# A hybrid attention trunk on one core: two products over the compressed probabilities on GpSimd, the block choice and its mask's transposition in other steps

## The reference, cut to what matters

```python
# compressed keys (63 of them): softmax, kept for the choice of blocks too
p_cmp = masked_softmax(s_cmp, cmp_mask)
o_cmp = einsum('bsghc,bcgd->bsghd', p_cmp, vcmp)
# block choice: probabilities summed over the 4 heads of a group, gathered
# to 16 blocks of 64 keys; 8 blocks are chosen by top-k
imp = einsum('bsgc,cn->bsgn', p_cmp.sum(axis=3), overlap)
imp = where(valid, imp + FORCE_BONUS * forced, -1.0)
_, sel_idx = lax.top_k(imp, 8)
# o_sel: softmax over the chosen blocks; o_w: over a window of 512 keys
o = g[:, :, 0] * o_cmp + g[:, :, 1] * o_sel + g[:, :, 2] * o_w
```

## Time and profile before

| what | value |
|---|---|
| median of 3 runs | 3226.2 us (3223.99 to 3230.59) |
| the profiled execution: its own time | 3225.85 us |
| the profiled execution: span from first to last instruction | 3224.1 us |
| PE busy, share of the span | 97% |
| DVE busy | 61% |
| POOL busy | 52% |
| ACT busy | 34% |
| mean granted TensorE clock | 0.993 |

### The profile page before, as it was taken

The page is one execution under the profiler, slowest core; times in us unless marked ns, Lnnn a source line. Parts: engine busy times, 40 slices in busy tenths (PEclk is TensorE's granted clock), DMA queues, the critical chain, the costliest instruction groups (busy, mean ns, idle before and its releaser), DMA issues.

```text
span 3224.1 us, 40879 instructions
## 1 busy us (share of the span) xinstructions
PE 3125.8 (97%) x15015; PEld 2551.7 (79%) x15045; DVE 1979.9 (61%) x2633; ACT 1098.7 (34%) x1993; POOL 1675.7 (52%) x1781
## 2 busy tenths in 40 slices
PE   8999999998999999999999999989989999999998
PEld 6888887676788888888778888867668888888887
DVE  7882256887656666655578532578765655555555
ACT  2124314666312222222220342356651222222233
POOL 3457632233463556666745585222334566666665
PEclk7999999999999999999999999999999999999999
DMA  7444541001522222211234457200115221111112
GB/s 256 147 159 131 159 117 27 1 1 34 176 85 79 79 79 71 74 53 53 79 131 137 144 154 188 66 1 1 34 33 177 69 82 53 53 52 49 51 46 105
DMA packets 301358, 280.99 MB, mean 87 GB/s; under 512 B 11115, under 2 KB 275559, under 8 KB 300648
## 3 DMA queue, kind: packets, MB, share of 16 engines
q1 hardware_dynamic: 282002, 212.90, 22.6%
q10 hardware_dynamic: 19158, 65.47, 5.5%
HBM read 232.20 MB, written 38.80 MB: 84 GB/s over the span
## 4 chain that ended last, share of the span: by engine, by line
PE 88%; DVE 8%; ACT 2%; issue 2%; POOL 1%; ACTq 0%; DVEq 0%; POOLq 0%
PE lin L1451 47%; PE lin L1881 16%; PE lin L1598 8%; PE aux L1740 2%; DVE pTL L2643 2%; PE pv L1756 2%; PE lin L1716 1%; DVE negm L2619 1%; PE pv L1757 1%; PE lin L1787 1%; PE lin L1717 1%; PE pv L1556 1%; ACT pTH L2203 1%; PE lin L1682 1%; PE lin L1501 1%
## 5 line engine op out<-in xcount | busy, mean ns | idle before, releaser
L1291 POOL TENSOR_SCALAR unit<-wraw 128x512 fp32r<-128x512 f32 x340 | 286.9, 844 | 775.2 <-PE lin L1451 270.6
L1451 PE MATMUL lin<-hH,unit 128*128 128x512 f32 x1824 | 577.8, 392 | 0.1
L1451 PE MATMUL lin<-hL,unit 128*128 128x512 f32 x1824 | 573.5, 390 | 0.0
L1451 PE MATMUL lin<-hH,wlo 128*128 128x512 f32 x1824 | 572.9, 390 | 0.0
L1293 POOL TENSOR_TENSOR wlo<-wraw,unit 128x512 fp32r<-128x512 f32 x340 | 490.7, 1443 | 28.4
L1881 PE MATMUL lin<-fH,unit 128*128 128x512 f32 x1568 | 486.8, 390 | 5.3 <-DVE xT L2778 5.3
L2778 DVE SCALAR_TENSOR_TENSOR xT<-lin,adac,xT 128x512 f32<-128x512 f32 x448 | 328.7, 748 | 182.7 <-PE lin L1881 178.1
L1451 PEld LDWEIGHTS lin<-hH,wlo 128*128 128x128 f32 x1824 | 342.8, 188 | 72.3
L1451 PEld LDWEIGHTS lin<-hL,unit 128*128 128x128 f32 x1824 | 342.9, 188 | 71.8 <-issue 0.2
L1451 PEld LDWEIGHTS lin<-hH,unit 128*128 128x128 f32 x1824 | 339.5, 188 | 70.1 <-issue 1.9
L1881 PEld LDWEIGHTS lin<-fH,unit 128*128 128x128 f32 x1568 | 294.3, 188 | 68.2 <-POOL unit L1326 3.9
(11 more groups left out here) (353 smaller groups left out, 5715.1 us busy)
## 6 DMA issues: line engine op xcount, KB each, us to landing
wraw<-in_w_ff SPq DMA_DIRECT2D x136, 512.0 KB, 4.0
wraw<-in_w_ada SPq DMA_DIRECT2D x80, 512.0 KB, 3.9
wraw<-in_w_in SPq DMA_DIRECT2D x72, 512.0 KB, 4.9
mix_keep<-tmp ACTq DMA_DIRECT2D x32, 512.0 KB, 6.2
wraw<-in_w_o SPq DMA_DIRECT2D x24, 512.0 KB, 4.3
adar<-in_w_ada SPq DMA_DIRECT2D x16, 512.0 KB, 11.9
x_keep<-xT ACTq DMA_DIRECT2D x4, 2048.0 KB, 9.3
gate_keep<-ropes ACTq DMA_DIRECT2D x16, 512.0 KB, 3.6
```

The source lines that it names most:

```text
L1291: pool.tensor_scalar(high, raw, 1.0, 1.0, ALU.mult, ALU.mult).then_inc(w_hi, 1)
L1451: mm = pe.matmul(lin[c % 2][:, hf], w, m(k, hf), start=first, stop=last)
```

## The change

`cmp_probs` on DVE keeps only the sum, the reciprocal and the small gate product, and signals a new semaphore, for every tile but 7. POOL makes the one or two products over the probabilities in a new function, `compressed`, three steps after the c unit. The memset and the sum over the heads move to `cmp_sums`, which `select` calls. `select` itself moves from two steps after the c unit to five steps after it. The b group of tiles 6, 5 and 4 moves from one step before the end of the tile's first w set to three steps before; that of tile 7 stays. Two semaphores count over both layers where they counted for one.

```diff
-            steps[e - 1].append(dict(kind="b", qt=s["qt"]))
+            steps[e - (1 if s["qt"] == NT - 1 else 3)].append(dict(kind="b", qt=s["qt"]))
...
+                def compressed(qt):
+                    nth, n = NTH[qt], SEEN[qt]
+                    c3, r8 = cprob[:, :, 0:n], cst[:, 2, :].rearrange("p (h o) -> p h o", o=1).to_broadcast([P, NH, n])
+                    gate = gates[:, qt, 0:NH].rearrange("p (h o) -> p h o", o=1).to_broadcast([P, NH, n])
+                    pool.wait_ge(c_recip, (NT - 1) * layer + nth)
+                    pool.wait_ge(t_done, C_GROUP[qt + 1, NKV - 1]["no"] + 1)
+                    if qt >= CHOICE:
+                        pool_then(pool, pool.tensor_tensor(c3, c3, r8, ALU.mult))
+                    pool.tensor_tensor(cgated[:, :, 0:n], c3, gate if qt >= CHOICE else r8, ALU.mult).then_inc(c_gated, 1)
...
                     for u in range(len(STEPS)):
+                        if u >= 3 and u - 3 < len(UNITS) and UNITS[u - 3][0] == "c":
+                            compressed(UNITS[u - 3][1])
...
                 def cmp_probs(qt):
...
-                    gate = gates[:, qt, 0:NH]
-                    if qt < CHOICE:
-                        then(dve.tensor_tensor(r8, r8, gate, ALU.mult))
-                        gate = r8
-                    else:
-                        then(dve.tensor_tensor(c3, c3, bc(r8, n), ALU.mult))
                     if NTH[qt]:
-                        dve.wait_ge(t_done, C_GROUP[qt + 1, NKV - 1]["no"] + 1)
-                    dve.tensor_tensor(cgated[:, :, 0:n], c3, bc(gate, n), ALU.mult).then_inc(c_gated, 1)
-                    if qt < CHOICE:
+                        if qt < CHOICE:
+                            then(dve.tensor_tensor(r8, r8, gates[:, qt, 0:NH], ALU.mult))
+                        dve.sem_inc(c_recip, 1)
                         return
+                    then(dve.tensor_tensor(c3, c3, bc(r8, n), ALU.mult))
+                    dve.tensor_tensor(cgated[:, :, 0:n], c3, bc(gates[:, qt, 0:NH], n), ALU.mult).then_inc(c_gated, 1)
+
+                def cmp_sums(qt):
+                    n = SEEN[qt]
+                    dve.wait_ge(c_gated, NTH[qt] + 1)
                     then(dve.memset(psum4[:, :, :], 0.0))
                     p4 = cprob.rearrange("p (g i) c -> p g c i", g=NKV)[:, :, 0:n, :]
                     then(dve.tensor_reduce(psum4[:, :, 1:1 + n], p4, AX.X, ALU.add))
                 def select(qt):
+                    cmp_sums(qt)
...
-                    if 2 <= u < len(UNITS) + 2 and UNITS[u - 2][0] == "c" and UNITS[u - 2][1] >= CHOICE:
-                        select(UNITS[u - 2][1])
+                    if 5 <= u < len(UNITS) + 5 and UNITS[u - 5][0] == "c" and UNITS[u - 5][1] >= CHOICE:
+                        select(UNITS[u - 5][1])
```

More of the change, by code:

```diff
@@ L527, in trunk @@
         fin_low, o_hi, fin_lo = sem("fin_low"), sem("o_hi"), sem("fin_lo")
+        c_exp, c_recip = sem("c_exp"), sem("c_recip")
         sq_made, ss_added, ss_done = sem("sq_made"), sem("ss_added"), sem("ss_done")
@@ L1112, in layer_programs @@
             s_done, max_made, exp_made = (lsem(s) for s in ("s_done", "max_made", "exp_made"))
-            c_in_made, c_exp, sel_made = (lsem(s) for s in ("c_in_made", "c_exp", "sel_made"))
+            c_in_made, sel_made = (lsem(s) for s in ("c_in_made", "sel_made"))
+            exp0 = NT * layer
             c_gated, t_done, v_done = (lsem(s) for s in ("c_gated", "t_done", "v_done"))
@@ L2549, in cmp_scores @@
                     if NTH[qt]:
-                        dve.wait_ge(c_exp, NTH[qt])
+                        dve.wait_ge(c_exp, exp0 + NTH[qt])
                     s3 = bank[:, 0:512].rearrange("p (h c) -> p h c", h=NH)[:, :, 0:n]
@@ L2558, in cmp_probs @@
                     c3 = cprob[:, :, 0:n]
-                    dve.wait_ge(c_exp, NTH[qt] + 1)
+                    dve.wait_ge(c_exp, exp0 + NTH[qt] + 1)
                     then(dve.tensor_reduce(sum8, c3, AX.X, ALU.add))
```

## The result

| | before | after |
|---|---|---|
| median | 3226.3 us (3223.99 to 3230.59, 4 runs) | 3245.0 us (3243.98 to 3247.16, 4 runs) |
| ratio | | 1.0061, 95% interval 1.0050 to 1.0073 |
| profiled execution: span | 3224.1 us | 3242.1 us |
| mean granted TensorE clock | 0.993 | 0.988 |

The changed kernel is slower by 18.7 us, 0.6%. A second measurement of the same kernel (the last experiment) gave 16.2 us, ratio 1.0046.

A forecast was written before the change was run, and what follows sets the result against it. PE was taken as the bound, busy for 97% of the span. Per layer -10.9 -0.9 +10.9 +0.9 +3.8 +3.2 = +7.0 us, two layers +14 us, so 3225.85 becomes 3240 us; range 3214 to 3250.

The forecast's parts named there:

- Part 1, the products leave DVE: On tiles 6, 5 and 4 PE's waits behind DVE's block of products and select go; gain 7.2 us per layer.
- The narrow tiles: Tiles 3 to 0 lose one DVE product each; gain 0.9 us per layer, bounds 0 and 2.5.
- Part 2, the mask: On tiles 6, 5 and 4 PE no longer waits for ACT's mask copy; gain 3.7 us per layer.
- Parts 3 and 4, the wait at b and POOL's series: b group of tiles 6, 5, 4 waits for its bank, 10.9 us per layer; select beside POOL's scaling adds 3.8.
- The "lighter steps", 0.9 us per layer: Steps 20 to 22 have less PE work than DVE work; new waits, 0.9 us per layer, bounds 0 to 2.
- Part 5, the clock: Clock falls behind each of six new PE waits of 4 to 5.5 us; 3.2 us per layer, bounds 0, 5.
- A sign that came without its consequence: The prediction is wrong if DVE's block starts before step 17's groups are done; no size given.
- The side of the covered wait: Rival: b waits some 1.7 us instead of 3.6, no clock fall; -6.4 per layer, 3213 us, chance 0.16.

The follow-up runs named there:

- The seventh experiment: The kernel before with only the b groups of tiles 6, 5 and 4 moved two steps earlier; 3221.2 us, ratio 0.9987.
- The third experiment: The changed kernel with the set's factors made behind select, so POOL's scalings start after it; 3229.8 us, ratio 1.0015.
- the fifth experiment: The changed kernel with 18 matmuls that add zero ahead of each b group of tiles 6, 5 and 4; 3229.6 us, ratio 1.0017.
- the sixth experiment: The changed kernel with the next step's scores issued on PE ahead of the b groups of tiles 6, 5 and 4; 3238.0 us, ratio 1.0041.

## Why the prediction was right, point by point

The forecast was 3240 us; the two medians are 3245.0 and 3241.7.

- **Part 1, the products leave DVE.** Right. PE's waits for DVE's banks outside b went from 7.4 us to 0.4. (Of the 7.4, 0.8 us and not 0.2 lay elsewhere, 0.19 and 0.61 at the end of tile 4. And the 4.8 us that DVE has less add up to 4.7 from their own parts; neither enters the sum.) On POOL the products took 0.92 us for 440 columns, not the estimated 1.2, and PE waited for none of them. The narrow tiles gave 1.8 us per layer instead of 0.9, inside the bounds.
- **Part 2, the mask.** Right: no row L1732 <- ACT selT is left on tiles 6, 5 and 4. The seventh experiment shows the move alone: with the block not in that step it costs 1.40 us per layer, at tile 4, and saves the 3.7.
- **Parts 3 and 4, the wait at b and POOL's series.** Right, place, releaser and size. The sum was 3.3 + 1.6, 3.2 + 1.2 and 4.4 + 1.0, so 4.9, 4.4 and 5.4 us; the profile has 4.87, 4.42 and 5.49. The third experiment shows the two halves apart: 3.19, 3.05 and 4.36 us without POOL. The pattern in `select` came as written as well: one operation waits, one slips in, one waits. L2602, now L2618, which it took into account with 0.2 us per tile beside the sum, lost 0.16, 0.05 and 0 us on tiles 6, 5 and 4.
- **The "lighter steps", 0.9 us per layer.** Wrong; no such waits are among PE's in the earlier trace rows's stretch after the change. With a full clock the wide part is 160.6 us (the fifth experiment) against 157.0 before, so 3.7 us more where the terms for it (-10.9, +10.9, +0.9 and +3.8) add up to 4.7.
- **Part 5, the clock.** The mechanism was right, the clock fell behind all six waits of 4.4 to 5.5 us. The size was off: 1.06 us for each, against 5.9 and 4.1 us per layer in one profile and 7.1 and 6.9 in another, so 1.4 to 2.4 us each. Three of these four lie above the term's own upper bound of 5 us, for which no row is given. The step that failed is the price taken from the earlier trace rows. There PE had worked 2.5 us of the 4 us ahead of the fall; here it had been idle for 4.4 to 5.5 us, resumed mostly at 1.2 GHz, and had dense work ahead at once. It then worked at that clock for 2.9 to 5.5 us behind each.
- **A sign that came without its consequence.** The prediction called itself wrong if DVE's block started before step 17's groups were done. It did: the block's reduction starts at 578.96 us (its memset at 578.76), and PE makes the second group of step 17 only from 579.12 on. The price came out all the same, since b's bank is freed in step 18 and the distance counts from the end of the block. The sign was badly chosen.
- **The side of the covered wait.** Its 5.4 us are not three times the 1.7 us it names (5.1); the waits of 4.87, 4.42 and 5.49 us rule it out either way.

For layer 0 of the profile after: +3.7 for the wide part, -1.8 for the narrow tiles, +5.9 for the clock, together +7.8 where +7.0 stood. Two errors that nearly cancel, the clock too small by 2.7 and the other terms too large by 1.9, make the forecast look better than its terms. (The profile before holds one fall per layer of its own, 1.06 us in the wide part of layer 0 and 1.2 in the narrow part of layer 1, and the one after holds a fall of 1.5 and 1.2 us in its narrow parts. With them the sum for layer 0 is 7.8 - 1.1 + 1.5 = 8.2 us and for layer 1 3.7 - 1.8 + 4.1 - 1.2 + 1.2 = 6.0, which are the 8.2 and 5.9 measured.)

**What the cause is.** Each of the three parts was taken back or done alone. The b group alone gains 4 us, with the block in its new step b's place hardly matters (3246.9 us), and the products on POOL gain. The loss is in the place of the block. It stands undivided, 4.7 us beside POOL's series, in a step in which DVE has nothing to spare: whatever group PE transposes next, b or the one after it, needs a bank that DVE frees only behind the block. Without POOL the whole block became a wait there (3.19 and 3.05 us on tiles 6 and 5, where b alone waits for nothing), while 1.6 to 1.8 us of waits were left where it stands two steps earlier: there some 1.4 us of it fit in unseen. Moving it there, with the products, is worth 24 to 27 us. The loss has three terms, each shown by its own experiment: the block's own time, POOL beside it (4.2 us per layer), and the clock behind it (4.1 to 7.1 us per layer).

**What stays open.** That the two measurements of the changed kernel differ by 2.5 us, and what of it is clock and what the spread of the other stretches. Equal waits, released at the same place of the program, cost 1.4 us each in one layer and 2.4 in another run, because the clock came back sooner or later, and one of 3.05 us was followed by a fall in one layer only; no experiment here tells what decides either.

## What to carry to other kernels

Before a block is moved on an engine that isn't the bound, ask what the bounding engine wants next from it there: put it in the step where that is wanted latest, and in two pieces in two steps rather than whole in one. Keep DVE's small operations, those with two SBUF inputs above all, away from a series on POOL; here the order of two calls, the factors last, was worth 13 to 16 us. Price a wait of several us on PE at its own length and the slow work behind it, here 1.4 to 2.4 us more each.

## What the runs showed of the hardware

- **The price of a clock fall depends on what PE has to do behind it.** It was 1.06 us in the earlier trace rows, and 1.4 to 2.4 us each, on average over a layer, behind the waits at b. Behind the waits of 3.65 us and more in the changed kernel and in the sixth experiment (1.2 GHz in their transpositions or right behind) it fell each time, behind four shorter ones (3.05 and 3.19 us) once. The price at b comes near half of the time that PE then worked at 1.2 GHz. In the earlier trace rows 0.57 granted over 4 us makes 1.7 us by the same estimate, and only 1.06 were lost. It mostly fell before PE resumed, as in the 0.66 of the wait's last 3 us. The Trainium skill (TensorE: Matmul & The Clock Gate, What's actually happening) has half rate as the state at rest and activity as what releases it. The trace agrees: PE idle for 4.87 us ahead of 0.50 granted, and 1.00 again from 591 us on, after dense work.
- **Filling is enough.** Matmuls that add zero kept the clock at 1.00 through the same delay of the bank, and brought back 12 to 14 of the 16 to 19 us.
- **Beside POOL's series only some of DVE's operations are held.** The reductions, the eight-maxima and replace operations kept their times. On tile 6 L2603 and the second L2606 took 1.00 and 0.91 us instead of 0.22 and 0.19, each until POOL's running multiplication was over, and the L2606 between them slipped in with 0.22. L2618, with one tensor input, took 0.34 us on tile 6, 0.23 on tile 5 and 0.18, its time alone, on tile 4. It too ended right behind POOL's last multiplication where it was held (583.68 after 583.64), so its loss is small because little of that was left. The Trainium skill (GPSIMD Engine Reference, Key points) names both kinds, two SBUF inputs and a 2-port mode. The rows agree on the first; in which mode L2618 ran, none of them shows.
